# A two-layer hybrid trunk on one core: the triangular inverse in two half chains of two chunks, its last level on 64 x 64 corner blocks, the small projection packed

## The reference

```python
h = rmsnorm(x, pre_norm)
proj = jnp.einsum('bld,de->ble', h, w_in)
(gq, gk, gv, gz, gb, ga, sx, sB, sC, sz, sdt, rq, rk, rv, rg) = split_cols(proj, IN_SIZES)
...
a_low = jnp.einsum('bihd,bjhd->bhij', kb, ki) * decay * strict
rhs = jnp.concatenate([vi * bi[..., None], kb * jnp.exp(gcum)[..., None]], axis=-1)
sol = lax.linalg.triangular_solve(a_low + eye, rhs, left_side=True, lower=True)
...
mixed = jnp.concatenate([o_a, o_b, o_c], axis=-1)
out = jnp.einsum('ble,ed->bld', mixed, w_out)
return x + rmsnorm(out, post_norm)
```

## Time and profile before

| | us |
|---|---|
| median of 3 runs | 2277.09 (2271.56 to 2277.39) |
| the profiled execution's own time | 2267.16 |
| its span | 2265.3 |
| PE busy | 2179.1 (96%) |
| DVE busy | 1339.4 (59%) |
| ACT busy | 878.5 (39%) |
| POOL busy | 499.7 (22%) |

### The profile page before, as it was taken

How to read it: one execution, slowest core, us unless ns; L and a number is a source line. 1 busy time by engine, 2 the same in 40 slices (tenths; PEclk the granted TensorE clock), 3 DMA queues, 4 the chain that set the end, 5 groups by cost and what they waited for, 6 DMA issues and landing times.

```text
span 2265.3 us, 38624 instructions
## 1 busy us (share of the span) xinstructions
PE 2179.1 (96%) x15412; PEld 1975.5 (87%) x15412; DVE 1339.4 (59%) x2436; ACT 878.5 (39%) x1759; POOL 499.7 (22%) x432
## 2 busy tenths in 40 slices
PE   7999989999999999999999999999999999999996
PEld 6887878999898798999988788889998888899996
DVE  5677567545476657523566776763456777555324
ACT  5444257323333317411343433663334333463101
POOL 3433324331010002100233333333210101021001
PEclk9999999999999999999999999999999999999998
DMA  6654456677463334455466444557676533444433
GB/s 232 230 191 154 158 176 207 226 258 261 155 243 121 112 114 148 165 170 183 165 222 240 175 162 165 202 184 254 227 246 199 204 112 112 140 144 155 168 122 149
DMA packets 98193, 410.84 MB, mean 181 GB/s; under 512 B 11168, under 2 KB 12256, under 8 KB 84192
## 3 DMA queue, kind: packets, MB, share of 16 engines
q1 hardware_dynamic: 97440, 407.98, 51.3%
q10 hardware_dynamic: 576, 0.40, 0.1%
HBM read 257.17 MB, written 151.16 MB: 180 GB/s over the span
## 4 chain that ended last, share of the span: by engine, by line
PE 82%; DVE 9%; issue 4%; ACT 3%; POOL 1%; DMA 0%; ACTq 0%; DVEq 0%; POOLq 0%
PE ps L1161 78%; PE ps L1164 4%; DVE wk L1630 2%; DVE wk L1644 1%; POOL w_low L2150 1%; DVE wk L1605 0%; DMA row<-in_rows 0%; DVE wk L1609 0%; DVE wk L1608 0%; DVE et L1566 0%; ACT w_hi L1878 0%; DVE wo_parts L1724 0%; POOL rs L2108 0%; DVE gss L1579 0%; DVE acc L1816 0%
## 5 line engine op out<-in xcount | busy, mean ns | idle before, releaser
L1161 PE MATMUL ps<-w_hi,hT_hi 128*128 128x256 f32 x1792 | 527.5, 294 | 3.2 <-DVE hT_lo L1480 3.2
L1161 PE MATMUL ps<-w_low,hT_hi 128*128 128x256 f32 x1792 | 508.5, 284 | 0.0
L1161 PE MATMUL ps<-w_hi,hT_lo 128*128 128x256 f32 x1792 | 502.8, 281 | 0.0
L2150 POOL TENSOR_TENSOR w_low<-w_loaded,w_hi 128x512 fp32r<-128x512 f32 x208 | 287.9, 1404 | 412.2 <-ACT w_hi L1878 412.1
L1161 PEld LDWEIGHTS ps<-wk 128*128 128x128 f32 x2336 | 296.8, 192 | 91.1 <-DVE wk L1630 22.5
L1161 PE MATMUL ps<-wk 128*128 128x128 f32 (+2 forms) x2336 | 344.7, 287 | 21.0 <-DVE wk L1657 5.3
L1161 PEld LDWEIGHTS ps<-w_low,hT_hi 128*128 128x128 f32 x1792 | 343.6, 192 | 2.8 <-issue 2.4
L1161 PEld LDWEIGHTS ps<-w_hi,hT_hi 128*128 128x128 f32 x1792 | 338.8, 189 | 6.6 <-DVE hT_lo L1480 3.8
L1161 PEld LDWEIGHTS ps<-w_hi,hT_lo 128*128 128x128 f32 x1792 | 342.6, 191 | 0.0
L1161 PE MATMUL ps<-hT_hi,w_hi 128*128 128x512 f32 x768 | 330.3, 430 | 7.2 <-POOL w_low L2150 4.9
L1161 PE MATMUL ps<-hT_lo,w_hi 128*128 128x512 f32 x768 | 303.4, 395 | 0.0
(11 more groups left out here) (197 smaller groups left out, 3183.4 us busy)
## 6 DMA issues: line engine op xcount, KB each, us to landing
w_loaded<-in_w_in SPq DMA_DIRECT2D x104, 512.0 KB, 5.0
w_split<-w_hi SPq DMA_DIRECT2D x52, 1024.0 KB, 6.9
w_split<-w_low SPq DMA_DIRECT2D x52, 1024.0 KB, 9.4
w_hi<-w_split SPq DMA_DIRECT2D x104, 512.0 KB, 6.3
w_low<-w_split SPq DMA_DIRECT2D x104, 512.0 KB, 7.2
wo_loaded<-in_w_out SPq DMA_DIRECT2D x32, 512.0 KB, 4.2
wk<-cum_rows SPq DMA_DIRECT2D x32, 512.0 KB, 4.4
wo_split<-wo_hi SPq DMA_DIRECT2D x32, 512.0 KB, 8.0
```

The costliest lines, as they stand in the source:

```text
L1161: return nc.tensor.matmul(o, a, b, start=start, stop=stop)
L2150: tt(w_lo[at], wr[at], w_hi[at], ALU.subtract)\
```

## The change

It does the following:
- **Half chains.** Each `gdn_p` and `gdn_xx` becomes two steps j = 0, 1 of two chunks each, with a PSUM bank and waits of their own. DVE's operations on them cover 256 columns instead of 512.
- **Corner blocks.** In the last level only the 64 x 64 block below the diagonal changes, so PE multiplies 64-row, 64-column blocks, and DVE copies and subtracts those alone; the mask is no longer applied there.
- **Small projection packed.** High and low weights lie side by side, so one matmul with 48 output rows takes the place of two with 24; `small_turn` adds the two while it turns, as a matmul with two stacked identities (`C_TWO`).
- **Order.** The planner's costs of these steps and its constants change; norms of tiles 2 and 3 stand after slices 3 and 7 of the first piece in each part; the next head's `gdn_decay` stands after the first chunk of the scan; the last group's `out` units run tp 0 of all units first; up to `KEEP` = 4 half units of the last part's third group are held back for the end; the last units' weights are placed in SP's list after those. At the start, DVE waits for `pars` alone and no longer for `rows`.

```diff
@@ mixing_steps
         for k in range(1, LEVELS):
-            out += [("gdn_p", p, h, k), ("gdn_xx", p, h, k)]
+            out += [(name, p, h, k, j) for name in ("gdn_p", "gdn_xx") for j in range(2)]
...
@@ make_plan
         if step[0] == "mix_turn":
-            outs.extend(("out", *step[1:3], u, tp) for u in range(UNITS) for tp in range(NT // 2))
+            if step[1:3] == (PARTS - 1, GROUPS - 1):
+                outs.extend(("out", *step[1:3], u, tp) for tp in range(NT // 2) for u in range(UNITS))
+            else:
+                outs.extend(("out", *step[1:3], u, tp) for u in range(UNITS) for tp in range(NT // 2))
...
+        if unit and unit[1:3] == (PARTS - 1, GROUPS - 2):
+            if front_at < len(front) and not stuck and len(outs) <= KEEP or front_at == len(front) and step and wait < HOLD:
+                unit = None
...
-OUT_WAIT = 2500
+OUT_WAIT = 3500
+KEEP = 4
+HOLD = 500
-NEAR = 120
+NEAR = 40
...
@@ loads of SP
         for u in range(UNITS):
-            loads.append((where["proj", PARTS - 1, len(PIECES) - 1, 1, Q - 1], u, ("tail", PARTS - 1, u)))
+            loads.append((max(where["proj", PARTS - 1, len(PIECES) - 1, 1, Q - 1], where["out", PARTS - 1, GROUPS - 2, UNITS - 1, 0]),
+                          u, ("tail", PARTS - 1, u)))
...
@@ PE, small
                     for kk in range(KD):
-                        mm(b, hi[:, kk, :], hT_hi[:, kk, :], kk == 0, False)
-                        mm(b, lo[:, kk, :], hT_hi[:, kk, :], False, False)
-                        i = mm(b, hi[:, kk, :], hT_lo[:, kk, :], False, kk == KD - 1)
+                        if kk:
+                            mm(b[0:NSM, :], both[:, kk - 1, 0], hT_lo[:, kk - 1, :], False, False)
+                        if kk == KD - 1:
+                            mm(b[0:NSM, :], both[:, kk, 0], hT_lo[:, kk, :], False, False)
+                        i = mm(b[0:2 * NSM, :], both[:, kk].rearrange("p e n -> p (e n)"), hT_hi[:, kk, :], kk == 0, kk == KD - 1)
...
@@ PE, gdn_p (gdn_xx alike)
-                    h, lv = s[2], s[3]
+                    h, lv, j = s[2:]
                     if lv == 1:
                         pe.wait_ge(S["gdn_xt"], GH * p + h + 1)
                     else:
-                        wait_emptied(pe, ("gdn_xx", p, h, lv - 1))
+                        wait_emptied(pe, ("gdn_xx", p, h, lv - 1, j))
                     b = opened(s)
-                    for c in range(NT):
-                        i = mm(b[:, c * P:(c + 1) * P], aT[:, c, :], X[:, c, :])
+                    for c in range(2):
+                        if lv < LEVELS - 1:
+                            i = mm(b[:, c * P:(c + 1) * P], aT[:, 2 * j + c, :], X[:, 2 * j + c, :])
+                        else:
+                            i = mm(b[64:P, c * 64:(c + 1) * 64], aT[0:64, 2 * j + c, 64:P], X[0:64, 2 * j + c, 0:64])
...
@@ DVE, gdn_p
-                        wait_emptied(dve, ("gdn_xx", *s[1:3], s[3] - 1))
-                        nc.vector.transpose(XT.rearrange("p c n -> p (c n)"), X.rearrange("p c n -> p (c n)")).then_inc(S["gdn_turned"], 1)
+                        wait_emptied(dve, ("gdn_xx", *s[1:3], s[3] - 1, s[4]))
+                        nc.vector.transpose(XT[:, own].rearrange("p c n -> p (c n)"), X[:, own].rearrange("p c n -> p (c n)")).then_inc(S["gdn_turned"], 1)
                     wait_filled(dve, s)
...
-                    empty(tt(PP, bank4(s), over_rows(mask), ALU.mult), s)
+                    if s[3] < LEVELS - 1:
+                        empty(tt(PP[:, own], bank4(s)[:, 0:2], over_rows(mask, 2), ALU.mult), s)
+                    else:
+                        corner = bank(s)[64:P, 0:P].rearrange("p (c n) -> p c n", c=2)
+                        empty(nc.vector.tensor_copy(PP[64:P, own, 0:64], corner), s)
```

More of the change, by code:

```diff
@@ L61 @@
 C_ZERO = C_PW2 + 8
-C_LEV = C_ZERO + 4
+C_TWO = C_ZERO + 4
+C_LEV = C_TWO + NSM
 C_DM = C_LEV + LEVELS * 128
@@ L94, in constants @@
     c[:, C_LEV:C_LEV + P] *= -1.0
+    c[:2 * NSM, C_TWO:C_LEV] = np.tile(np.eye(NSM), (2, 1))
     c[:, C_PW:C_PW + 8] = -0.5
@@ L178, in front_steps @@
                         add(("scale", p + 1, 2 + (q > 3)))
[L179 to L182, removed]
+                    if (i, half) == (0, 0) and q in (3, 7):
+                        add(("norm", p, 2 + q // 4), ("rescale", p, 2 + q // 4))
                     if (i, half, q) == (0, 1, 3):
@@ L410, in play @@
             mark("n", both(700, "a"))
-            mark(("xt", p, r[0], 1), both(640, "n"))
-            mark(("x", p, r[0], 1), dve(600))
+            mark("n", both(640, "n"))
+            mark("n", dve(600))
+            for j in range(2):
+                at["xt", p, r[0], 1, j] = at["x", p, r[0], 1, j] = at["n"]
             mark(("kq", p, r[0]), pool(1400))
@@ L417, in play @@
         elif k == "gdn_p":
-            h, lv = r
+            h, lv, j = r
             if 1 < lv < LEVELS - 1:
-                mark(("xt", p, h, lv), dve(600, *after))
-            mark("n", pe(4 * LINE))
-            mark(("pp", p, h, lv), dve(640, "n"))
+                mark(("xt", *step[1:]), dve(370, *after))
+            mark("n", pe(2 * LINE))
+            mark(("pp", *step[1:]), dve(380, "n"))
             if lv == LEVELS - 1:
                 after = []
-                mark("n", pe(4 * TURN))
-                mark(("xt", p, h, lv), act(560, "n"))
+                mark("n", pe(2 * TURN))
+                mark(("xt", *step[1:]), act(340, "n"))
         elif k == "gdn_xx":
-            h, lv = r
-            mark("n", pe(4 * LINE))
-            mark(("x", p, h, lv + 1) if lv < LEVELS - 1 else ("xt", p, h, LEVELS), dve(640, "n"))
+            h, lv, j = r
+            mark("n", pe(2 * LINE))
+            mark(("x", p, h, lv + 1, j) if lv < LEVELS - 1 else ("xt", p, h, LEVELS, j), dve(380, "n"))
         elif k == "gdn_s":
@@ L1624, in _ @@
                 elif k == "gdn_xx":
-                    h, lv = s[2], s[3]
+                    h, lv, j = s[2:]
+                    own = slice(2 * j, 2 * j + 2)
                     wait_filled(dve, s)
@@ L1843, in _ @@
             for l in range(DEPTH):
-                act.dma_start(row[:, l, :], rows[l].partition_broadcast(P)).then_inc(pars_in, 16)
+                act.dma_start(row[:, l, :], rows[l].partition_broadcast(P)).then_inc(rows_in, 16)
             for s in plan:
```

74 lines of the change are left out of this document (39 added, 35 removed).

## The result

| | before | after |
|---|---|---|
| median | 2275.88 us (2271.56 to 2277.39, 4 runs) | 2202.15 us (2199.71 to 2203.35, 4 runs) |
| ratio, 95% interval | | 0.9678, 0.9661 to 0.9694 |
| span of the profiled execution | 2265.3 us | 2199.7 us |

73.7 us less, where 46 were forecast: the time lies 11 us under the low end of the range. The direction was right, the size was not.

A forecast was written before the change was run, and what follows sets the result against it. The prediction took TensorE's work plus its stops, mainly waits for VectorE in the inverse, as the bound. Its terms summed to -46 us, from 2277 to 2231 us; forecast 2218 to 2243, full range 2213 to 2254.

The forecast's parts named there:

- Half chains: Inverse steps: splitting them removes most of TensorE's 97 stops of about 0.25 us for VectorE, -18 us (bounds 0 and -24).
- Corner blocks: Last level of the inverse: 64x64 instructions save 6 us; later copies in ten of 16 heads cost 3.
- Small projection: TensorE's small projection: 32 fewer matmuls of 512 columns at 0.23 us, with nothing to hide it, -7.5 us.
- three quarters of the 24: Inverse: share of 24 us of TensorE's stops taken as gain, since convolution taps still stop it sometimes; -18 us.
- Room before the first mix_turn: Parts 0 and 2, late gates: six slices fill the hole, -7 us, and less granted clock is lost, -1.
- Norms: Part starts: norms 2 and 3 placed later let slices cover two waits for a rescaled tile, -4 us.
- Start: Kernel start: VectorE's first product no longer waits for the rows, -1 us.
- Tail: Kernel end: held-back half units -4 us, weights queued behind residual loads +3, earlier final of rows 0 and 1 -2.5.
- 1: Rival: VectorE's half operations in the inverse cost 0.56 us and take back the 18; 2249 us, chance 0.17.
- 2: Rival: a half operation on VectorE takes as long as a whole one, 0.69 us; slower, 2289 us, chance 0.07.
- 3: Rival: corners give 14, the chain all 24, the clock holds; 16 us more gain, 2215 us, chance 0.13.
- 4: Rival: the new order makes holes at the tail's weights or the front's wait for POOL's split; 2255 us, chance 0.13.

The follow-up runs named there:

- merged_same_order: The kernel after with the two halves of each inverse step (levels 1 to 6) joined into one step at the second half's place: 2243.8 us.
- turns_first: The kernel after with TensorE, in the last level, turning X of both halves before the corner products of both: 2198.6 us.

## Why the prediction was wrong, by its steps

- **Half chains, -18 (bounds 0 and -24): the step that failed.** In the order of after they are worth 42 us (merged_same_order). "97 stops of about 0.25" took the gap of 0.24 for the price. The price is 0.36, because the weight load behind a wait is in the open. And "three quarters of the 24" was too careful for this order: VectorE's half operation is 0.40 to 0.43, so a level is 2 x (0.43 + 0.40 + 0.42) + 0.56 = 3.06 us of 3.16, and only 14 stops are left. The mechanism was right, and so was the reading of the earlier trace rows. With the old constants 50 stops stay and the halves bring some 25 of the 35 measured: the term had no room for what the order does for the halves.
- **A term that was missing: the decay's place, 35 us in after** (alone 21, some 10 of them the pace). It is described in the change and priced at nothing. The view of waits of before had ScalarE standing 74.7 us for it. I went by what TensorE waits for, and the weight loads wait only 6.3 us for `w_low`; what the held splits would cost once the plan changes I did not follow.
- **A difference that nobody priced: the pace, some 10 us.** Undisturbed 256-column matmuls start 0.1190 us apart in before and 0.1179 in after. Its cause is open.
- **The constants, no term either: 20.7 us in after**, 7 on halves alone. That a planner takes a half step only when its inputs are there was not in the sum.
- **Corner blocks, -6 and +3:** nothing to be told from zero. Pitch 0.059 as in the best bound, given back at the changes of shape.
- **Small projection, -7.5:** 0.8, not to be told from nothing. The 32 matmuls are gone, and TensorE is busy 6.5 us less for it. "With nothing to hide it" failed: 3.8 us reappear as longer waits.
- **Room before the first mix_turn, -7 and -1:** the gate is waited for 4.2 instead of 5.33, twice, so 2.2 us. The six slices are there. VectorE's timeline after shows why the wait stays: two more taps of the convolution than before stand in front of the gate and take 2.58. The return of the clock, -1, is not separated.

```profile
288.59 2.58 DVE L1544 SCALAR_TENSOR_TENSOR slot<-raw,par,slot 128x512 f32<-128x512 f32 x2
...
292.31 1.50 DVE L1719 TENSOR_TENSOR gate<-gate,ss 128x512 f32<-128x512 f32 x1
```

- **Norms, -4:** 8.5. **Start, -1:** the first slice starts at 14.22 where it did at 15.63, right. **Tail, -4, +3, -2.5:** one wait of 3.97 for one of 4.3, and the last matmul starts 12.2 us before the end instead of 14.0: about -2 in sum, the order of events as forecast.
- **Rivals.** 1 and 2 (VectorE takes it back) are refuted by 0.40 to 0.43 per half operation. 3 had the right sign and was 13 us short. 4 came true in part, at the tail and at the gates; the front's wait for GpSimd's split did not grow (5.6 us of `w_low`, 6.3 before).

The sum was 28 us too small. Too low were the halves (by 23 in the order of after) and the norms (by 4.5), and decay, constants and pace had no term; corners, packing, room and tail were put too high by some 17. The measured parts do not add up to a division of the 74, since they act on each other. That the miss is no larger is luck: terms too low and terms too high stand against each other.

## What to carry to other kernels

Price a wait in front of a matmul by a whole step with and without it, not by its gap: the weight load comes on top (0.36 us instead of 0.24 here). Of every step that a change moves, look up who waits for its result on every engine, and what stands queued behind that engine, even where TensorE's own waits name somebody else. Where a list is laid out greedily, test parts together: one part was worth 0, some 11 or 35 us depending on the rest. And compare the pace of undisturbed instructions before giving a difference to the parts: here some 10 us came with all variants alike, and a variant with the new table of constants alone would have been the baseline to measure from.

## What was not expected of the hardware

- A tile of 64 rows and 64 columns starts 0.059 us after the last one, but only in a run of its kind: each change of the weights' shape costs 0.09 us on the way in, also where only the columns differ (128 x 64). Two runs of four and one of eight break even with full blocks (2.73 us a level against 2.76); two runs of eight (turns_first) make the level 0.44 us shorter.
- 64 rows by 128 columns are no faster than full weights: 0.112 us each, and the change-over on top: 14 us more than after.
- Undisturbed matmuls of 256 columns start 0.1190 us apart in one program and 0.1179 in nineteen others, and an undisturbed stretch shows it at a granted clock of 1.00 in both; it is some 10 us of 2200. What sets it is not known.
